# Attention probabilities of a two-block kernel turned by VectorE and through DRAM, not by TensorE

## The reference

```python
for l in range(DEPTH):                                   # DEPTH = 2
    h = einsum('bsd,de->bse', x, w_in[l]) + b_in[l]      # 1024 -> 4864
    q, k, v, z_a, u_g, v_g, z_g, g_a, g_g = split_columns(h)
    y_a = sliding_window_attention(q, k, v, sinks[l]) * silu(z_a)   # 8 heads of 64, 2 for k and v
    y_g = chunked_spatial_gating(gelu(u_g), gelu(v_g), ...) * silu(z_g)
    merged = sigmoid(g_a) * (y_a @ w_branch_attn[l]) + sigmoid(g_g) * (y_g @ w_branch_gmlp[l])
    x = layer_norm(ALPHA * x + merged @ w_out[l] + b_out[l], ...)
```

## Time and profile before

| what | value |
|---|---|
| median of 3 runs (lowest, highest) | 1551.63 us (1551.46, 1552.85) |
| the profiled execution, whole time | 1552.21 us |
| its span in the profile | 1550.5 us |
| PE busy (matmuls) | 1540.2 us, 99% |
| PE busy (weight loads) | 1381.8 us, 89% |
| DVE, ACT, POOL busy | 65%, 38%, 23% |
| granted TensorE clock, mean | 0.999 |
| DMA | 149.78 MB, 97 GB/s in the mean |

### The profile page before, as it was taken

One profiled execution on the slowest core, in us unless ns is written; L12 is line 12 of the kernel. 1 busy time (PEld: TensorE's weight loads), 2 busy tenths in 40 slices (PEclk: granted clock), 3 DMA queues, 4 the chain that ended last, 5 costly groups with the idle time before them and its releaser, 6 DMA issues.

```text
span 1550.5 us, 29971 instructions
## 1 busy us (share of the span) xinstructions
PE 1540.2 (99%) x12487; PEld 1381.8 (89%) x12487; DVE 1005.7 (65%) x1654; ACT 592.1 (38%) x1070; POOL 356.5 (23%) x333
## 2 busy tenths in 40 slices
PE   9999999999999999999999999999999999999998
PEld 9999999999999899899998898888888988888886
DVE  6656565775877678586786677567516786576346
ACT  5323232253444344334444445482112346541121
POOL 0000000020421214042142124334530043343510
PEclk9999999999999999999999999999999999999999
DMA  5322322323332523423243142222324322222331
GB/s 170 110 82 91 101 82 82 110 82 96 105 103 64 134 59 111 119 75 95 72 112 125 55 135 91 75 80 93 97 82 143 122 82 82 82 82 82 117 128 55
DMA packets 124722, 149.78 MB, mean 97 GB/s; under 512 B 4812, under 2 KB 100464, under 8 KB 124592
## 3 DMA queue, kind: packets, MB, share of 16 engines
q1 hardware_dynamic: 120880, 143.17, 30.1%
q10 hardware_dynamic: 3632, 4.53, 0.9%
q0 software_dynamic: 80, 0.20, 0.1%
HBM read 141.33 MB, written 6.55 MB: 95 GB/s over the span
## 4 chain that ended last, share of the span: by engine, by line
PE 98%; DVE 1%; DMA 0%; issue 0%; ACT 0%; SPq 0%; POOL 0%; ACTq 0%; DVEq 0%; POOLq 0%
PE acc L409 28%; PE acc L411 28%; PE acc L410 28%; PE aux L569 1%; PE aux L409 1%; PE aux L411 1%; PE aux L410 1%; PE aux L629 1%; PE aux L631 1%; PE aux L1391 1%; PE aux L1421 1%; PE aux L621 1%; PE aux L550 1%; PE aux L1410 1%; PE aux L1411 0%; PE aux L1445 0%
## 5 line engine op out<-in xcount | busy, mean ns | idle before, releaser
L409 PE MATMUL acc<-xhis,whi 128*128 128x264 f32 (+2 forms) x1848 | 611.3, 331 | 0.0
L411 PE MATMUL acc<-xhis,wlo 128*128 128x264 f32 (+2 forms) x1848 | 602.1, 326 | 0.0
L410 PE MATMUL acc<-xlos,whi 128*128 128x264 f32 (+2 forms) x1848 | 601.8, 326 | 0.0
L411 PEld LDWEIGHTS acc<-xhis,wlo 128*128 128x128 f32 x1848 | 347.9, 188 | 29.2
L409 PEld LDWEIGHTS acc<-xhis,whi 128*128 128x128 f32 x1848 | 348.0, 188 | 28.9 <-issue 0.3
L410 PEld LDWEIGHTS acc<-xlos,whi 128*128 128x128 f32 x1848 | 348.3, 188 | 26.8
L404 POOL TENSOR_TENSOR wlo<-raw,whi 128x1024 fp32r<-128x1024 f32 x84 | 207.7, 2473 | 377.0 <-DVE whi L2533 377.0
L400 ACT ACTIVATE whi<-raw 128x1024 fp32r<-128x1024 f32 x158 | 164.1, 1048 | 133.4 <-PE acc L411 119.2
L404 DVE TENSOR_TENSOR wlo<-raw,whi 128x1024 fp32r<-128x1024 f32 x81 | 99.8, 1235 | 36.9 <-ACT whi L400 36.7
L2230 DVE TENSOR_TENSOR wlo<-raw,whi 128x1024 fp32r<-128x1024 f32 x77 | 93.7, 1218 | 21.9 <-ACT whi L400 21.7
L2533 DVE CAST whi<-raw 128x1024 fp32r<-128x1024 f32 x84 | 66.8, 797 | 54.0 <-PE acc L411 53.8
(11 more groups left out here) (390 smaller groups left out, 2781.0 us busy)
## 6 DMA issues: line engine op xcount, KB each, us to landing
raw<-in_w_in SPq DMA_DIRECT2D x38, 1024.0 KB, 5.3
raw<-in_hgrn_w_in SPq DMA_DIRECT2D x32, 1024.0 KB, 6.4
raw<-in_pool_w_in SPq DMA_DIRECT2D x15, 1024.0 KB, 5.5
raw<-in_pool_w_out SPq DMA_DIRECT2D x8, 1024.0 KB, 5.1
raw<-in_hgrn_w_out SPq DMA_DIRECT2D x8, 1024.0 KB, 5.3
raw<-in_w_out SPq DMA_DIRECT2D x8, 1024.0 KB, 5.1
v_turn<-vb SPq DMA_DIRECT2D x8, 544.0 KB, 7.6
raw<-in_pool_w_grp SPq DMA_DIRECT2D x4, 1024.0 KB, 5.2
```

The source lines that it names most:

```text
L409: pe.matmul(dst, stat[0], mov[0], start=first, stop=False)
L410: pe.matmul(dst, stat[0], mov[1], start=False, stop=False)
L411: return pe.matmul(dst, stat[1], mov[0], start=False, stop=last)
```

## The change

The probabilities are no longer turned by PE. In its place:

- DVE turns them in blocks of 32 by 32, two instructions in each step, at the end of `att_vector` for block s-1, into one of three buffers `pb` (that lie in `sqs`, `xns` and `kf`).
- ACT issues a transfer of `pb` to a tensor in DRAM, `p_turn` (128 partitions, 512 numbers each, 256 KB), at step s for block s-2.
- ACT issues four transfers back, each to 32 partitions of `pt` (64 KB each, in runs of 128 numbers), that put the blocks of 32 in their places. They stand behind the exponentials of step max(t+3, 4*(t//4)+4) for block t: two blocks at steps 4, 8, 12 and 16, and one at 5, 6, 9, 10, 13, 14, 17 and 18.
- The products with the values stand behind steps 8, 12, 16 and 19 (`VALUES_AT`), not 6, 10, 14 and 18, and so do DVE's product with `za`, `yah` and `yal`. They wait for `pt_landed`.
- ACT's copy L1828 and PE's 112 turns L1421 are gone. `pt` has the same size, and its rows are read in another order by the products with the values.

```diff
+        pb = [rows[:, 0:SEQ].rearrange("p (b n j) -> p b n j", b=4, n=4) for rows in (sq[1], xn[1], kf)]
...
+        VALUES_AT = {8: 0, 12: 1, 16: 2, 19: 3}
+        p_turn = nc.dram_tensor("p_turn", (len(ATT), P, SEQ), F32).ap()
...
             def att_tensor(i, s):
                 base = 16 * i
-                for t in range(s - 6, s - 2) if s >= 6 and s % 4 == 2 else ():
+                for t in range(4 * VALUES_AT[s], 4 * VALUES_AT[s] + 4) if s in VALUES_AT else ():
                     p, b = ATT[t]
-                    pe.wait_ge(apt_ready, 1 + base + t + 1)
+                    if b == 0:
+                        pe.wait_ge(pt_landed, 64 * (base + t + 4))
...
-                if 2 <= s < len(ATT) + 2:
-                    t = s - 2
-                    b = ATT[t][1]
-                    pe.wait_ge(aprob, 3 * (base + t) + 3)
-                    pe.wait_ge(apt_ready, 1 + base + t)
-                    for x in range(2):
-                        for kb_ in range(0 if b else 1, 2):
-                            mm = pe.transpose(aux2[:, 0, P * (2 * x + kb_):P * (2 * x + kb_ + 1)],
-                                              pr[t % 2][:, x, P * kb_:P * kb_ + P], ident[:, :])
-                    mm.then_inc(apt_full, 1)
...
             def att_scalar(i, s, between=None):
                 base = 16 * i
-                if 2 <= s < len(ATT) + 2:
-                    t = s - 2
-                    z, first = t % 2, (0 if ATT[t][1] else 1)
-                    act.wait_ge(apt_full, base + t + 1)
...
-                    act.activation(pt[t % 4][:, :, :].rearrange("p (x k) q -> p x k q", x=2)[:, :, first:, :],
...
                 if between is not None:
                     between()
+                if 2 <= s < len(ATT) + 2:
+                    n = base + s - 2
+                    act.wait_ge(pb_ready, 2 * n + 2)
+                    act.dma_start(p_turn[s - 2], pb[n % 3].rearrange("p b n j -> p (b n j)")).then_inc(pb_sent[n % 3], 16)
                 if s < len(ATT):
                     lo, z = (0 if ATT[s][1] else P), s % 2
                     act.wait_ge(arow, base + s + 1)
...
+                for t in range(len(ATT)):
+                    if s == max(t + 3, 4 * (t // 4) + 4):
+                        n = base + t
+                        act.wait_ge(pb_sent[n % 3], 16 * (n // 3) + 16)
+                        if t == 2:
+                            act.wait_ge(res_ready, 4 * i + 4)
+                        if n >= 4:
+                            act.wait_ge(ao_full, base + 4 * (t // 4))
+                        blocks = p_turn[t].rearrange("(a p) n -> p a n", a=4)
+                        for b in range(4):
+                            act.dma_start(pt[t % 4][32 * b:32 * b + 32, :, :, :].rearrange("p a n j -> p a (n j)"),
+                                          blocks[:, :, P * b:P * b + P]).then_inc(pt_landed, 16)
...
+                if 1 <= s < len(ATT) + 1:
+                    t = s - 1
+                    first, z = (0 if ATT[t][1] else 1), t % 2
+                    dve.wait_ge(aprob, 3 * (base + t) + 3)
+                    n = base + t
+                    if n >= 3:
+                        dve.wait_ge(pb_sent[n % 3], 16 * (n // 3))
+                    for x in range(2):
+                        dve.transpose(pb[n % 3][:, :, 2 * x + first:2 * x + 2, :].rearrange("p b k j -> p k b j"),
+                                      pr[z][:, x, P * first:2 * P].rearrange("p (k b j) -> p k b j", b=4, j=32))\
+                           .then_inc(pb_ready, 1)
```

More of the change, by code:

```diff
@@ L270, in program @@
                 brow = sb("brow", [P, D], where=in_rows)
-            pt_more = [sb(f"pt{s}", [P, 4, P], where=before_g) for s in (2, 3)]
+            pt_more = [sb(f"pt{s}", [P, 4, 4, 32], where=before_g) for s in (2, 3)]
         gac = sb("gac", [P, 4, SEQ], where=in_c)
@@ L290, in program @@
             pr = [sb(f"pr{s}", [P, 2, 2 * P + 1], where=before_m) for s in range(2)]
-            pt = [sb(f"pt{s}", [P, 4, P], where=before_m) for s in range(2)] + pt_more
+            pt = [sb(f"pt{s}", [P, 4, 4, 32], where=before_m) for s in range(2)] + pt_more
             sgc = [xn[0][:, 0:SEQ], rstd[:, 0:SEQ]]
@@ L354, in program @@
         aexp, aprob, sink_ready = sem("aexp"), sem("aprob"), sem("sink_ready")
-        apt_full, apt_ready, ao_full = sem("apt_full"), sem("apt_ready"), sem("ao_full")
+        pb_ready, pb_sent = sem("pb_ready"), [sem(f"pb_sent{n}") for n in range(3)]
+        pt_landed = sem("pt_landed")
+        ao_full = sem("ao_full")
         ya_ready, yahi_ready, yalo_ready = sem("ya_ready"), sem("yahi_ready"), sem("yalo_ready")
@@ L844, in c_slots @@
                         att += 1
-                    elif att < len(ATT) + 3 and att >= len(ATT):
+                    elif att <= max(VALUES_AT) and att >= len(ATT):
                         side.append(("att", att))
@@ L1570, in _ @@
         def _(act):
-            act.sem_inc(apt_ready, 1)
             act.sem_inc(on_ready, 1)
@@ L1819, in att_scalar @@
                 base = 16 * i
-                if 2 <= s < len(ATT) + 2:
-                    t = s - 2
-                    z, first = t % 2, (0 if ATT[t][1] else 1)
-                    act.wait_ge(apt_full, base + t + 1)
-                    if t >= 4:
-                        act.wait_ge(ao_full, base + t - 3)
-                    if t == 2:
-                        act.wait_ge(res_ready, 4 * i + 4)
-                    act.activation(pt[t % 4][:, :, :].rearrange("p (x k) q -> p x k q", x=2)[:, :, first:, :],
-                                   aux2[:, 0, :].rearrange("p (x k q) -> p x k q", x=2, k=2)[:, :, first:, :],
-                                   ACT.Copy).then_inc(apt_ready, 1)
                 if between is not None:
                     between()
+                if 2 <= s < len(ATT) + 2:
+                    n = base + s - 2
+                    act.wait_ge(pb_ready, 2 * n + 2)
+                    act.dma_start(p_turn[s - 2], pb[n % 3].rearrange("p b n j -> p (b n j)")).then_inc(pb_sent[n % 3], 16)
                 if s < len(ATT):
@@ L1835, in att_scalar @@
                     act.wait_ge(arow, base + s + 1)
+                    if i and s < 2:
+                        act.wait_ge(pb_ready, 2 * (base + s - 1))
                     for x in range(2):
@@ L1839, in att_scalar @@
                            .then_inc(aexp, 1)
-                if s >= 3 and ATT[s - 3][1] == CH - 1:
-                    p = ATT[s - 3][0]
+                for t in range(len(ATT)):
[10 more added lines that the diff above has]
+                                          blocks[:, :, P * b:P * b + P]).then_inc(pt_landed, 16)
+                if s in VALUES_AT:
+                    p = VALUES_AT[s]
                     act.wait_ge(ya_ready, 1 + 4 * i + p + 1)
-                    act.activation(yah[:, p, :], sq[p % 2][:, 0:SEQ], ACT.Copy).then_inc(yahi_ready, 1)
+                    act.activation(yah[:, p, :], sq[0][:, 0:SEQ], ACT.Copy).then_inc(yahi_ready, 1)
             for i in range(DEPTH):
@@ L2465, in att_vector @@
                     dve.tensor_reduce(sm[z][:, 0, :], sc[z][:, :, lo:], AX_X, ALU.max, negate=True).then_inc(arow, 1)
-            def att_gate(i, s):
-                if s >= 3 and ATT[s - 3][1] == CH - 1:
-                    p = ATT[s - 3][0]
-                    dve.wait_ge(ao_full, 16 * i + s - 2)
-                    dve.tensor_tensor(sq[p % 2][:, 0:SEQ], aux2[:, 1, :], za[:, p, :], ALU.mult)\
+                if 1 <= s < len(ATT) + 1:
[9 more added lines that the diff above has]
+                           .then_inc(pb_ready, 1)
+            def att_gate(i, s):
+                if s in VALUES_AT:
+                    p = VALUES_AT[s]
+                    dve.wait_ge(ao_full, 16 * i + 4 * p + 4)
+                    if 4 * i + p:
+                        dve.wait_ge(yahi_ready, 4 * i + p)
+                        dve.wait_ge(yalo_ready, 4 * i + p)
+                    dve.tensor_tensor(sq[0][:, 0:SEQ], aux2[:, 1, :], za[:, p, :], ALU.mult)\
                        .then_inc(ya_ready, 1)
             def att_vector_out(i, s):
-                if s >= 3 and ATT[s - 3][1] == CH - 1:
-                    p = ATT[s - 3][0]
+                if s in VALUES_AT:
+                    p = VALUES_AT[s]
                     dve.wait_ge(yahi_ready, 4 * i + p + 1)
-                    dve.tensor_tensor(yal[:, p, :], sq[p % 2][:, 0:SEQ], yah[:, p, :], ALU.subtract)\
+                    dve.tensor_tensor(yal[:, p, :], sq[0][:, 0:SEQ], yah[:, p, :], ALU.subtract)\
                        .then_inc(yalo_ready, 1)
```

2 lines of the change are left out of this document (1 added, 1 removed).

## The result

The changed kernel takes 1556.84 us (median of 9 runs, 1555.90 to 1557.84), the kernel before beside it 1551.94 us (9 runs, 1551.46 to 1553.08). The ratio is 1.0030, with a 95% interval of 1.0021 to 1.0038: slower by 4.9 us. The forecast was slower by 18.4 us, 1570; the time lies inside its range, near the low end. The direction was right and the size was not, by nearly four times.

A forecast was written before the change was run, and what follows sets the result against it. The time was taken as the sum of what PE executes. Per layer, 15.6 us of new waits less 6.15 gained give +9.4, twice +18.9 on 1552.2: 1571.1, stated as 1570 us, range 1553 to 1587.

The forecast's parts named there:

- The gain: PE loses 112 turns at 0.11 us each: 12.3 us, 6.15 in each layer.
- cover: Part of ACT's load issues that goes beside the exponentials: 0.6 of their 1.1 us, between 0.2 and 1.0.
- The forecast's own walk: Count through one layer of four places where ACT or a transfer ends last: 15.6 us of new PE waits.
- A: u into vg: ACT reads u's units late, so PE waits 3.4 us before vg's first product.
- B: vg into zg: DVE's additions free the first slot late; PE waits 1.8 us, 0.7 if DVE is not late.
- C: zg: DVE frees `aux` late; PE waits 5.5 us for the scores of step 14, another 1.9 next round.
- D: Loads land late: PE waits 1.7 us at step 16, 0.2 at 12, 1.1 at 19; 3.0 a layer.
- bounds: The same walk with low and high prices for issue, cover and landing: 1547.5 and 1584 us.
- the faster rival: "Faster: the issues take no time from ACT", whose sequencer runs ahead: 1543 us, chance 0.12.
- ring: zg: ACT's sigmoid, DVE's product, scaling, adding, ACT's exponentials, two tables; 6.0 us a round, no slack to PE's 5.93.
- No change: Rival: issues of 0.36 to 0.45 us, landing in 3.3, waits of some 6 us a layer: 1551, chance 0.05.
- Slower by far: Rival: transfers are the limit, landing in 5.5 to 6.3 us with little cover: 1585 us, chance 0.19.

The follow-up runs named there:

- the first experiment: The kernel before with PE's 112 turns left out and nothing in their place: 1539.81 us, ratio 0.9916.
- the last experiment: The changed kernel with SP issuing the transfers and the products with the values after steps 6, 10, 16 and 19: 1540.84 us, ratio 0.9926.
- fourth experiment: The changed kernel with ten unused products of 512 columns on PE ahead of the scores of step 14: 1555.21 us, ratio 1.0021.
- eleventh experiment: The changed kernel with DVE's turns moved behind its cast of the next weights: 1555.13 us, ratio 1.0023.
- seventh: The changed kernel with DVE's turns made twice, 0.7 us more in each step: 1564.92 us, ratio 1.0082.
- third: The changed kernel with values behind steps 7, 11, 15, 19 and each block's loads at step t+3: 1572.83 us, ratio 1.0136.

## Why the prediction was right in direction and wrong in size

**The gain.** 12.3 us forecast, 12.4 measured by the first experiment. Right. The new order of numbers that the values' products read costs nothing that can be seen: some 1.0 us is left in the last experiment for that and all else.

**What an issue costs ACT: the step that failed.** The forecast had "four loads cost ACT 1.85 us, eight cost 4.3", out of 0.61 us for an issue and 0.6 of cover. Measured are 0.76 and 3.0 us in the median (0.76 and 2.97 at steps 5 and 4 of the first layer), out of 0.45 for an issue and 1.03 of cover. Both prices were wrong in the same direction. The 0.61 came from SP's loads of the same form, whose shortest was 0.56; I kept only the 0.36 of ACT's own queue as a low end, though the earlier trace rows shows 0.49 there as well, and the three issues ahead of that one took 0.44 to 0.48. The cover was in the earlier trace rows too: there the issue started 0.01 us behind the *start* of the activation ahead of it, and that rule, taken for both exponentials, gives the whole 1.03. I took half of it without a row that asked for it.

The forecast's own walk, done again with 0.76 and 3.0 for the loads and 2.1 to land, gives A 1.0, B 0.7, C 4.0 and D nothing: 5.7 us in a layer, an estimate from these measured prices, against 6.3 and 5.7 measured. So the walk holds and its prices didn't. But 5.7 - 6.15, twice, is -0.9: with the right prices the same walk says 1551 us, no change. The kernel is slower by what the walk had no term for, the clock first of all. **That the direction came out right was luck**: waits that were forecast too long stood in for costs that weren't forecast.

**A, B, C.** The mechanism holds at each place, shown by the waits' names and by their going when ACT doesn't issue or issues less. The sizes in a layer: A 3.4 forecast, 1.2 and 1.5 measured; C 5.5 + 1.9 forecast, 2.4 + 1.7 and 3.3 + 0 measured. The 1.7 stands behind the one place where four loads stopped ACT as long as forecast (1.91 us, at step 13 of the first layer, where two of the issues took 1.94 together and two 0.94). B 1.8 forecast, 0.9 measured in all kernels with the values at step 8, whoever issues: DVE was not late there, and the 0.7 that the forecast gave for that case is near it. The experiment with values at step 6 has no such wait, which shows that it is the moved values' price: 2.6 us of the whole with the 0.8 for `ug`. At the two ends of the bounds the forecast's C is not what its walk gives: done again it comes to 2.3 and 8.6 us, not 3.0 and 7.8, and in the faster rival to 0.1, not 0.7. That moves these times by 1 to 2 us and no conclusion.

**D, the landing.** 3.0 us in a layer forecast, none measured: it took 2.1 us, not 4.5. The forecast kept between the 3.3 and 5.5 of the earlier trace rows, whose loads are twice as large; the shortest landing here is 1.8. The longest, 5.3, shows that the far end exists, but at no place that PE waited for.

**The clock.** In no step of the forecast. It costs some 2.6 us by the profile (1.6 by the fourth experiment), in the second layer alone.

**DVE's turns.** Costed at nothing, "hidden, unless DVE is late for another reason". That reason was there: in a ring without slack 0.7 us more of turns costs 8.1 us, and moving the turns out of POOL's way gives some 1.7, at the edge of the noise. With SP as issuer the same turns make PE wait nowhere.

**The account.** Waits 12.0, less 12.3, and 2.6 for the clock are 2.3 of the 5.6 us between the spans. A standstill costs more than its wait: from the last score product at 979.32 to the next product at 980.81 are 1.49 us, against 0.12 without a wait, so 1.37 for a named 1.21; over the seven of them that is about 1.1 us. Waits elsewhere in the program, which differ from one execution to the next, are 0.5 more in the changed kernel's profile (0.7 against 0.2 for `xt`). Some 1.7 us, a thousandth of the time, stay open.

**The rivals.** "Faster, the issues take no time from ACT" fell, with the threshold that it named: four loads cost 0.76, not under 0.6. "No change" (issues of 0.36 to 0.45, landing in 3.3, some 6 us of waits in a layer) described the trace best, with 0.45, 2.1 and 6.3: it had a chance of 0.05 and was off by 5 us: the clock, the standstills' tails, and what stays open. "Slower by far" didn't come about.

## What to carry to other kernels

Here a transfer cost the engine that issued it in so far as its issues outlasted what executed ahead of them: count issues, not bytes, and put them on an engine that no ring waits for; the same loads were worth -8.0 us on SP and +4.9 us on ACT. When an operand is bounded from two rows, walk the whole schedule at both, and add what a standstill does to the clock, since a ring without slack hands a stop on almost whole (3.99 us on ACT, 3.29 on PE). And moving work to another queue needs a look at both ends: at the waits that it now stands behind (8.7 us behind a piece of the weights), and at the waits that it leaves behind (a table load fell behind one).

## What the runs showed of the hardware

- In these traces ACT's DMA issues pass an activation that is in line, but not one that still waits for a semaphore: the store starts at 973.61 while the table loads and the reading of the unit starts only at 974.84; the loads start at 969.70, 0.02 us behind an exponential that had waited for DVE. The Trainium skill (Perfetto Trace Analysis, DVE / Act Engine Instruction) has the sequencer free for the next instruction as soon as one is in the wait queue. The first row agrees; the second shows a limit that it doesn't name.
- An issue over 32 partitions took 0.45 us, over 64 partitions 0.60, over all 128 partitions 0.33 (medians, ACT's queue), for 64, 128 and 256 KB; the first in runs of 512 bytes, the two others in runs of 2 KB.
- The length of a standstill alone doesn't say whether the granted clock falls. It was at 1.2 GHz for 3 to 7 us around the end of waits of 3.29 us (changed kernel), 3.02 and 3.52 (eleventh experiment), 2.84, 3.15 and 4.14 (seventh), and also after one of 2.05 (third). It stayed at 2.4 GHz after 2.44 us (changed kernel), 2.41 (third) and 3.05 (seventh), though in this last case it fell at the next wait, of 1.82 us, 8 us later. Ten products whose results nobody reads, put ahead of the wait, kept it up (fourth experiment).
- The two scalings of 128x256 numbers on DVE took 0.62 us together when alone, and 2.78 us when POOL's 2.40 us subtraction had begun 0.03 us before. The Trainium skill (SBUF — State Buffer, Who interferes with whom) says that a DVE operation in a two-port mode and one of GpSimd share a pair of ports as an exclusive lock, so that the second fully blocks until the first has finished. The trace agrees in size: 2.78 is about 2.40 and one more scaling of 0.31; in which mode DVE ran, no row shows.
